# GpSimd in place of VectorE makes the low parts of sixteen weight units of one projection

## What is computed

```python
hx = modulate(rms_norm(x, norm1_g[l]), mod_x[0], mod_x[1])
zx = jnp.split(hx @ w_in[l], N_PARTS, axis=-1)        # hc, zc: the same for the context
...
def token_mixers(z, k1, k2, v, ...):
    a_val, a_gate, q, _, _, u, sv, bg, cg, xin = z
    y_a = conformer_conv(a_val, a_gate, ...)          # gate, 31 taps, layer norm, silu
    y_b = diff_attention(q1, q2, k1, k2, v, ...)      # softmax 1 - lambda * softmax 2
    y_c = spatial_gating(u, sv, ...)
    y_d = short_conv_mixer(bg, cg, xin, conv_d_w)
    return jnp.concatenate([y_a, y_b, y_c, y_d], axis=-1) @ w_out
x = x + mod_x[2] * token_mixers(...)
x = x + mod_x[5] * channel_mixer(...)                 # relu squared, 1024 -> 4096 -> 1024
```

## Time and profile before

| | |
|---|---|
| median of 3 runs | 2528.37 us |
| lowest and highest of them | 2525.51 and 2531.92 us |
| the profiled execution, its own time | 2532.04 us |
| its span in the trace | 2530.3 us |
| TensorE busy | 2415.2 us, 95% |
| VectorE busy | 1655.7 us, 65% |
| ScalarE busy | 990.1 us, 39% |
| GpSimd busy | 30.6 us, 1% |
| granted TensorE clock, mean | 0.975 of full speed |

### The profile page before, as it was taken

One profiled execution on the slowest core, in us unless ns is written; L12 is line 12 of the kernel. 1 busy time (PEld: TensorE's weight loads), 2 busy tenths in 40 slices (PEclk: granted clock), 3 DMA queues, 4 the chain that ended last, 5 costly groups with the idle time before them and its releaser, 6 DMA issues.

```text
span 2530.3 us, 30801 instructions
## 1 busy us (share of the span) xinstructions
PE 2415.2 (95%) x12108; PEld 1942.4 (77%) x12108; DVE 1655.7 (65%) x2686; ACT 990.1 (39%) x1536; POOL 30.6 (1%) x64
## 2 busy tenths in 40 slices
PE   7999999999999999999999998999999999878997
PEld 3878877866687888877668997666788888757997
DVE  7776566444478886768568677686775454576654
ACT  2322322245534322224445444555431332455543
POOL 0000000010000000000000000000000000000000
PEclk9999999999999999999999999999999999978999
DMA  8355435541352444433314553212245344222653
GB/s 318 103 205 196 167 133 200 191 175 67 110 190 84 150 175 166 148 138 105 113 51 137 189 187 102 67 51 75 103 164 200 129 171 141 80 84 84 200 182 119
DMA packets 95803, 357.16 MB, mean 141 GB/s; under 512 B 10969, under 2 KB 11353, under 8 KB 93353
## 3 DMA queue, kind: packets, MB, share of 16 engines
q1 hardware_dynamic: 93082, 339.37, 38.5%
q0 software_dynamic: 2576, 15.82, 1.7%
HBM read 349.90 MB, written 5.24 MB: 140 GB/s over the span
## 4 chain that ended last, share of the span: by engine, by line
PE 71%; issue 16%; DVE 8%; ACT 3%; DMA 1%; POOL 0%; SPq 0%; POOLq 0%; DVEq 0%; ACTq 0%
PE PS L527 58%; PE PS L689 3%; PE PS L861 2%; PE PS L555 1%; DVE w_lo L1579 1%; PE PS L1021 1%; PE PS L803 1%; PE PS L802 1%; PE PS L812 1%; DMA ada_ring<-in_ada 1%; DVE conv L2216 1%; PE PS L705 0%; ACT w_hi L1046 0%; DVE xv L1972 0%; DVE h_lo L1962 0%
## 5 line engine op out<-in xcount | busy, mean ns | idle before, releaser
L1579 DVE TENSOR_TENSOR w_lo<-raw,w_hi 128x1024 fp32r<-128x1024 f32 (+1 forms) x456 | 543.2, 1209 | 354.6 <-ACT w_hi L1046 353.8
L1046 ACT ACTIVATE w_hi<-raw 128x1024 fp32r<-128x1024 f32 (+1 forms) x456 | 460.8, 1041 | 487.6 <-PE PS L527 476.8
L527 PE MATMUL PS<-h_hi,w_hi 128*128 128x512 f32 (+1 forms) x1528 | 525.9, 344 | 20.1 <-DVE h_lo L1962 10.3
L527 PE MATMUL PS<-h_lo,w_hi 128*128 128x512 f32 (+1 forms) x1528 | 522.2, 342 | 0.0
L527 PE MATMUL PS<-h_hi,w_lo 128*128 128x512 f32 (+1 forms) x1528 | 521.5, 341 | 0.0
L527 PEld LDWEIGHTS PS<-h_hi,w_hi 128*128 128x128 f32 x1528 | 288.8, 189 | 64.8 <-issue 13.3
L527 PEld LDWEIGHTS PS<-h_hi,w_lo 128*128 128x128 f32 x1528 | 288.9, 189 | 36.1
L527 PEld LDWEIGHTS PS<-h_lo,w_hi 128*128 128x128 f32 x1528 | 289.1, 189 | 34.8 <-issue 0.2
L527 PE MATMUL PS<-hid_hi,w_hi 128*128 128x512 f32 (+1 forms) x864 | 293.0, 339 | 2.4 <-DVE w_lo L1579 2.4
L527 PE MATMUL PS<-hid_lo,w_hi 128*128 128x512 f32 (+1 forms) x864 | 292.2, 338 | 0.0
L527 PE MATMUL PS<-hid_hi,w_lo 128*128 128x512 f32 (+1 forms) x864 | 292.2, 338 | 0.0
(11 more groups left out here) (360 smaller groups left out, 3469.3 us busy)
## 6 DMA issues: line engine op xcount, KB each, us to landing
raw<-in_weights SPq DMA_DIRECT2D x434, 512.0 KB, 4.5
ada_ring<-in_ada SPq DMA_DIRECT2D x176, 512.0 KB, 3.8
raw<-in_weights SPq DMA_DIRECT2D x22, 384.0 KB, 4.1
qk<-in_ada SPq DMA_DIRECT2D x4, 1024.0 KB, 11.3
xv<-in_ada SPq DMA_DIRECT2D x4, 1024.0 KB, 13.3
m_hi<-h_spill POOLq DMA_DIRECT2D x4, 1024.0 KB, 8.2
wgt<-in_x SPq DMA_DIRECT2D x2, 1024.0 KB, 22.7
h_spill<-h_hi POOLq DMA_DIRECT2D x1, 2048.0 KB, 8.3
```

The lines of the kernel that those rows point to most:

```text
L527: mm = pe.matmul(out, a, b, start=(k == 0 and i == 0), stop=(k == ph.k_tiles - 1 and i == 2))
L1046: act.activation(w_hi[:, s, 0:w], raw[:, s, 0:w], ACT.Copy).then_inc(sem("w_hi"), 1)
L1579: dve.tensor_tensor(w_lo[:, s, 0:w], raw[:, s, 0:w], w_hi[:, s, 0:w].bitcast(F32), ALU.subtract)\
```

## The change

The low parts of the sixteen units of `z0` are made by GpSimd, by the same subtraction on the same tiles, and counted by a new semaphore `pool_split`. The counts of `w_split` behind those units are lower by sixteen. All waits of TensorE and SP for a unit's low part go through two small functions that choose semaphore and count. The second mixer's `z1` stays with DVE.

```diff
+POOL_UNITS = range(LIN["z0"].u0, LIN["wo0"].u0)
...
+        def split_by(u):
+
+            return "pool_split" if u in POOL_UNITS else "w_split"
+
+        def split_count(u):
+
+            return u - POOL_UNITS[0] + 1 if u in POOL_UNITS else u + 1 - len(POOL_UNITS) * (u > POOL_UNITS[0])
...
                 if u >= RING:
-                    sp.wait_ge(sem("w_split"), u - RING + 1)
+                    sp.wait_ge(sem(split_by(u - RING)), split_count(u - RING))
...
+                for u in POOL_UNITS if l == 0 else ():
+                    s, w = w_slot(u), A["units_width"][u]
+                    pool.wait_ge(sem("w_hi"), u + 1)
+                    pool.tensor_tensor(w_lo[:, s, 0:w], raw[:, s, 0:w], w_hi[:, s, 0:w].bitcast(F32), ALU.subtract)\
+                        .then_inc(sem("pool_split"), 1)
             pool.wait_ge(sem("final"), 8)
...
-                        pe.wait_ge(sem("w_split"), u + 1)
+                        pe.wait_ge(sem(split_by(u)), split_count(u))
...
                     u = nsplit[0]
                     s, w = w_slot(u), A["units_width"][u]
+                    if u in POOL_UNITS:
+                        nsplit[0] += 1
+                        continue
                     dve.wait_ge(sem("w_hi"), u + 1)
```

## The result

The change makes the kernel slower, by little: 2535.56 us median against 2530.45 us for the kernel before (20 runs each), a ratio of 1.0017 with a 95% interval from 1.0009 to 1.0024. The medians differ by 5.1 us and the means by 4.3, so some 4 us were lost where 2 were forecast as gained. The profiled execution took 2532.72 us.

The account below looks back on a forecast made before the run. TensorE bounds the kernel, busy 2415 of 2530 us, idling in z0 partly behind DVE's queue. With full exclusion 2.44 + 0.3 - 0.3 - 0.3 = 2.1 us gained brings the median of 2528.37 to 2526.3 us, range 2520 to 2535.

Parts of the forecast that it names:

- What bounds the stage: z0 stage: TensorE idles 14.1 of 160 us, partly behind DVE's subtractions; removing them gives 6.2 us if nothing replaces them.
- rival without interference: DVE's taps and GpSimd's subtractions run side by side: 6.2 us gained plus up to 1.8 of clock, 2520.5 to 2522.2; chance 0.30.
- Tile 2: Maxima start 3.5 us earlier, so both idle stretches behind tile 3 go: 2.44 us gained, even under full exclusion.
- Exclusion: GpSimd's subtractions hold DVE's taps and differences for their whole length: gain 2.1 us instead of 6.2; chance 0.50.
- The price of one GpSimd subtraction: 1024 columns with two inputs on GpSimd: 1.94 us taken, bounds 1.06 and 4.0 us.
- 0.6 us for each 0.1 us: Each 0.1 us more per GpSimd subtraction delays the taps at tiles 4, 8 and 10 by 0.2 us each.
- Which DVE instructions are held: Taps and differences, reading two SBUF operands, are held by GpSimd for 3.9 us; maxima read PSUM and go on.
- the sign that was to decide between the cases: Tile 4's three taps: 2.33 us if the engines don't meet, over 3 us or a gap ahead if they do.
- TensorE's clock: Clock of 0.91 from 1680 to 1700 us, worth 1.8 us, counted only as a gain if the engines don't interfere.
- The slow rival: GpSimd is slow and holds DVE: a loss from 2.3 us per subtraction on, 2530 to 2543 us; chance 0.12.
- The base: Whole kernel before the change: median taken as 2528.37 us, from which the gain was subtracted.
- The costs set at nothing: TensorE waiting for GpSimd's low parts, SP's reloads and GpSimd's queue in the z0 stage: no cost.

Follow-up runs that it names:

- no_low: Changed kernel with the low parts of z0's sixteen units left out, high parts taken twice: stage 147.7 us, ratio 0.9953 against before.
- beside_sub: Kernel before, with GpSimd in addition doing sixteen unused subtractions of 1024 columns: stage 181.9 us, ratio 1.0086 against before.
- beside_set: Kernel before, with GpSimd in addition filling an unused tile three times by memset behind each of the sixteen roundings: stage 157.6 us, single run.
- halves: Changed kernel with each GpSimd subtraction cut into two of 512 columns: stage 157.8 us, single run.
- first_six: Changed kernel with only the first six units' low parts on GpSimd, the other ten on DVE: stage 154.5 us, ratio 0.9988 against before.

## Why the prediction was wrong

**What bounds the stage**: right. DVE's subtractions at tiles 2, 4, 8 and 10 stood ahead of TensorE's stretches, and without them the stage is 7.4 us shorter (no_low), where the working had 6.2 us of idle time (5.5 measured) and, in its rival without interference, up to 1.8 of clock (1.9 measured).

**Tile 2**: right, 2.28 of 2.44 us. GpSimd's pair runs while DVE does nothing that it holds, but for the scaling of the maxima (1.23 us for 0.17).

**Exclusion**: the right choice among the two, on thin evidence. beside_sub, beside_set and halves show it row by row: 6.80 us for a pair of 2.36, no hold of an instruction with two SBUF inputs beside mere writes, one instruction at a time. The Trainium skill (SBUF — State Buffer, Who interferes with whom) has it that "**A DVE instruction with two SBUF inputs contends with a GpSimd instruction that reads SBUF**, not with one that only writes it", and these rows agree.

**The price of one GpSimd subtraction** failed: 1.94 us was taken, 2.37 measured. The estimate scaled a one-input instruction of another kind. By the prediction's own 0.6 us for each 0.1 us this is 2.6 us. Measured: the stretches behind tiles 5, 9 and 11 changed by +0.87, +0.61 and +1.09 us where -0.3, +0.3 and +0.3 stood, 2.3 us in all. This step alone took back the 2.1 us of gain, and the idle time grew by 0.3 us instead. The estimate of 2.25 us from the Trainium skill (GPSIMD Engine Reference, section 3.1, Elementwise), which stood beside the sum, was nearer.

**Which DVE instructions are held** was incomplete. The working named the taps and the differences. The scaling of the maxima and the first tap of each half are `tensor_scalar` with one SBUF input, and it let them go on; they were held by up to 2.2 us each. That cost little more, since the taps behind them were held anyway: at tile 4 the first tap had to run after GpSimd's pair and not beside it, some 0.3 us. It also spoiled the sign that was to decide between the cases: the three taps of tile 4 took 2.33 us, with no gap ahead, as if the engines did not meet, because the hold stood in the two rows ahead of them.

**TensorE's clock** is the larger failed step: it made 3.1 us of the 0.3. The working named the clock as a gift in the rival without interference, and charged nothing for it in the forecast, though the 2.34 us stretch had the clock at 0.91 behind it. In the trace of before, the stretch of 1.86 us has full clock behind it, and the one of 2.34 us has not the earlier trace rows. Tile 5's stretch grew from 1.86 to 2.73 us, and the clock fell to 0.91 behind it (behind 2.35 us in halves too); tile 11's grew from 2.34 to 3.43 us, with 0.83 in place of 0.91. A stretch that grows should have been charged with the risk of 1.8 us (0.09 of 20 us) or twice that. It is a risk and not a price, since the length alone does not decide, as the last section shows.

**The slow rival** was priced with a threshold of 2.3 us for any loss: the measured 2.37 lies just past it, and the idle sum, 0.3 us longer, agrees with that. Its span from 2530 to 2543 us, with a chance of 0.12, holds the measured 2535.56, but not for its reason: at 2.37 us its own price gives a loss of some 0.5 us, and the clock, which it did not count, made the rest.

**The base** was off by luck. The median of three runs was 2528.37 us and that of twenty 2530.45, so 2.1 of the 9.3 us between the forecast 2526.3 and the measured 2535.56 have nothing to do with the change.

**The costs set at nothing**, TensorE waiting for a low part, SP's reloads, the queue on GpSimd, were nothing: no idle stretch of TensorE in the stage ends with a weight. No stretch came behind tile 6 or 12 either.

## What to carry over

In these traces, moving an elementwise instruction from DVE to GpSimd freed DVE only where DVE's neighbours in time read PSUM or wait, and not where they have two SBUF inputs or are a `tensor_scalar` from SBUF to SBUF. There DVE paid GpSimd's length in place of its own, here 2.37 us for 1.21; so choose the places by what DVE does there, not by how idle GpSimd is.

Sum idle time of TensorE in two columns: how much there is, and behind how many stretches the clock falls. A change that leaves the first alone can still lose by the second, and idle-filling products ahead of known waits (3.6 us here, with nothing else changed) may be worth more than the change itself.

## What the runs showed that was not expected

- A `tensor_scalar` on 128 x 2 numbers took up to 2.33 us (0.17 alone) when it met GpSimd's subtraction, and 0.4 to 0.7 us when it met a memset.
- Two engines that shut each other out take turns by instruction: DVE's pair of 2.36 us took 6.80 us, GpSimd's pair of 4.75 us took 6.75 us.
- A GpSimd subtraction of 512 columns takes 1.26 us (four in 5.03 us), one of 1024 columns 2.37 us, a memset of 1024 columns 0.95 us.
- The length of an idle stretch does not by itself tell whether TensorE's clock falls behind it. Stretches of 2.34 and 2.35 us, before and in first_six, have a clock of 0.91 and 0.83 in the 20 us from 1680 on. In beside_sub the clock fell behind a stretch of 1.59 us, where 1.86 us in before and 1.95 us in beside_set left it at full; in beside_set it stayed up behind 3.61 us, at the end of the stage, where it fell in before and after. First two rows of beside_sub, then two of beside_set:

```profile
1660.01 0.66 PE L950 MATMUL PS<-ident,probs 128*128 128x128 f32 x4 [1.59 <-DVE probs L2278]
...
1661.71 0.63 PE L870 MATMUL PS<-h_lo,w_hi 128*128 128x512 f32 x1
```

```profile
1737.99 1.10 PE L975 MATMUL PS<-xv,drot 128*128 128x512 f32 x2 [3.61 <-ACT xv L1078]
...
1739.40 0.39 PE L1036 MATMUL PS<-h_hi,w_lo 128*128 128x512 f32 x1
```

The runs don't tell what sets that; with the stretches filled it did not fall in the stage at all.
